# First mixture of experts: the up weights of a block in one 2 MB transfer

## The reference, cut to what matters

```
def expert_block(args):
    xb, ei = args
    hb = jax.nn.silu(xb @ w_gate[ei]) * (xb @ w_up[ei])      # 1024 -> 2 x 256
    return hb @ w_down[ei]                                   # 256 -> 1024
```

## Time and profile before

| | us |
|---|---|
| median of 3 runs | 2119.38 |
| lowest, highest | 2119.03, 2122.65 |
| span of the profiled execution | 2122.0 |
| PE busy in it | 1911.1 (90%) |
| DVE, ACT, POOL busy in it | 809.4, 501.7, 246.8 |

### The profile page before, as it was taken

The page is one execution under the profiler, slowest core; times in us unless marked ns, Lnnn a source line. Parts: engine busy times, 40 slices in busy tenths (PEclk is TensorE's granted clock), DMA queues, the critical chain, the costliest instruction groups (busy, mean ns, idle before and its releaser), DMA issues.

```text
span 2122.0 us, 26341 instructions
## 1 busy us (share of the span) xinstructions
PE 1911.1 (90%) x10372; PEld 1177.0 (55%) x10372; DVE 809.4 (38%) x1399; ACT 501.7 (24%) x868; POOL 246.8 (12%) x185
## 2 busy tenths in 40 slices
PE   9899999999989988999998998797978889797986
PEld 7777897785545567888987343332433333343433
DVE  5676454344634557558855110110201110120113
ACT  6656563331212145221224000000000000000002
POOL 4561520001111020003401000000000000000000
PEclk9999999989999999999999999999999999999999
DMA  7443441077999973312163999999999999999995
GB/s 292 159 157 138 184 157 60 1 289 303 421 423 422 417 299 127 129 57 100 60 258 138 418 417 421 413 422 412 422 416 419 419 415 422 412 421 413 421 416 198
DMA packets 123755, 630.67 MB, mean 297 GB/s; under 512 B 11708, under 2 KB 28476, under 8 KB 69021
## 3 DMA queue, kind: packets, MB, share of 16 engines
q1 hardware_dynamic: 109068, 598.65, 69.9%
q10 hardware_dynamic: 11216, 18.61, 2.3%
q0 software_dynamic: 3392, 12.32, 1.5%
HBM read 608.83 MB, written 20.71 MB: 297 GB/s over the span
## 4 chain that ended last, share of the span: by engine, by line
PE 53%; DMA 30%; DVE 6%; ACT 5%; POOL 2%; issue 2%; SPq 1%; POOLq 0%; ACTq 0%; DVEq 0%
PE psum L914 52%; DMA arena<-in_w 16%; DMA ring<-in_w 6%; DMA ring<-in_moe 4%; DMA in_spectra<-ring 2%; DVE arena L2216 2%; PE psum L912 1%; DVE weights_low L2208 1%; ACT weights_high L1754 1%; DVE arena L2208 1%; DMA arena<-in_stream 1%; ACT arena L1795 1%; SPq L614 1%; DMA arena<-x_rows,row_of 1%; ACT arena L1736 1%
## 5 line engine op out<-in xcount | busy, mean ns | idle before, releaser
L914 PE MATMUL psum<-ring,arena 128*64 128x512 f32 (+1 forms) x3064 | 688.3, 595 | 116.1 <-DMA ring<-in_w 87.3
L914 PEld LDWEIGHTS psum<-ring,arena 128*64 128x64 f32 x3064 | 227.9, 137 | 530.9 <-issue 522.0
L914 PE MATMUL psum<-arena 128*64 128x512 f32 (+5 forms) x1506 | 290.7, 457 | 28.5 <-DMA arena<-in_w 20.9
L1736 ACT ACTIVATE arena<-psum 128x512 f32<-128x512 f32 (+2 forms) x152 | 82.3, 550 | 722.6 <-PE psum L914 691.3
L914 PEld LDWEIGHTS psum<-arena 128*64 128x64 f32 (+2 forms) x1506 | 155.6, 166 | 171.6 <-issue 157.1
L914 PE MATMUL psum<-arena_low,weights_high 128*128 128x512 f32 (+1 forms) x704 | 249.3, 373 | 0.0
L914 PE MATMUL psum<-features_high_part,weights_high 128*128 128x512 f32 x576 | 228.3, 396 | 8.8 <-DVE weights_low L2208 3.0
L914 PE MATMUL psum<-features_high_part,weights_low 128*128 128x512 f32 x576 | 225.9, 392 | 0.0
L2216 DVE SCALAR_TENSOR_TENSOR arena<-psum,modp,arena 128x512 f32<-128x512 f32 x64 | 48.1, 751 | 319.2 <-PE psum L914 314.0
L2208 DVE TENSOR_TENSOR arena<-psum,arena 128x512 f32<-128x512 f32 (+2 forms) x48 | 28.9, 603 | 331.1 <-PE psum L914 255.5
L2208 DVE TENSOR_TENSOR weights_low<-ring,weights_high 128x2048 fp32r<-128x2048 f32 (+1 forms) x47 | 108.8, 2318 | 91.4 <-ACT weights_high L1754 87.8
(11 more groups left out here) (315 smaller groups left out, 1866.2 us busy)
## 6 DMA issues: line engine op xcount, KB each, us to landing
ring<-in_w SPq DMA_DIRECT2D x288, 1024.0 KB, 23.0
arena<-in_w SPq DMA_DIRECT2D x96, 1024.0 KB, 24.0
ring<-in_moe SPq DMA_DIRECT2D x93, 1024.0 KB, 20.3
ring<-in_stream SPq DMA_DIRECT2D x53, 1024.0 KB, 6.6
arena<-in_stream SPq DMA_DIRECT2D x16, 1024.0 KB, 4.9
in_spectra<-ring ACTq DMA_DIRECT2D x8, 1024.0 KB, 27.2
ring<-in_spectra SPq DMA_DIRECT2D x8, 1024.0 KB, 5.9
y_places<-arena ACTq DMA_DIRECT2D x15, 512.0 KB, 8.5
```

Source lines behind the costliest of these rows:

```text
L914: ins_ = pe.matmul(o, lhs, rhs, start=start, stop=stop)
L1736: bk.emptied.inc(act.activation(dst, o, func, **more))
```

## The change

The gate and up weights of a block come in one transfer of 2 MB instead of two of 1 MB. The array in HBM is the same. Seen as 256 rows of 8192 bytes (two halves of 128), partition q now takes rows 2q and 2q + 1, 16384 bytes in one run. Partition q < 64 so holds channels of the first four slices, and q >= 64 of the last four; which channel a partition holds is another one than before. To match it, `block_turned` picks every second channel of a slice (stride 2) and makes 16 products with the identity, 64 weight columns each, in place of eight transposes.

The nine slots become three of 2 MB for up weights and three of 1 MB for down weights, each with semaphores of its own (`s_upin`, `s_downin`). Block n waits for block n - 3 of its kind. SP's order in pair p is: the up weights of both blocks, then the down weights of the pair before. PE gives the slots of both blocks back when all of `up(p)` is done; `block_in(p + 2)` waits for that too. The filter tables are issued ahead of block 3's up weights. `moe1_uses` works out at which count of uses each block has been used. In pair 0 two small products follow `up`.

```
+    for e in range(experts_of(p)):
+        if 2 * p + e == UP_SLOTS:
+            filter_in()
+        up_in(2 * p + e)
     if p:
         for e in range(experts_of(p - 1)):
-            load(moe1_w[expert(p - 1, e), 2])
+            down_in(2 * p - 2 + e)
...
+def up_in(block):
+    if block >= UP_SLOTS:
+        sp.wait_ge(s_used, TURN["hyin"] + UP_USED[block - UP_SLOTS])
+    rows_ = moe1_w[expert(block), 0:2].rearrange("u p n -> (u p) n").rearrange("(q s) n -> q (s n)", s=2)
+    sp.dma_start(up_slot(block), rows_).then_inc(s_upin[block % UP_SLOTS], 16)
+    used.n += 1
+def down_in(block):
+    if block >= DOWN_SLOTS:
+        sp.wait_ge(s_used, TURN["hyin"] + DOWN_USED[block - DOWN_SLOTS])
+    sp.dma_start(down_slot(block), moe1_w[expert(block), 2]).then_inc(s_downin[block % DOWN_SLOTS], 16)
+    used.n += 1
...
 def block_turned(p):
-    k = 4 * half + j
-    mm(o[:, P * j:P * j + held], x_blk[p % 2][0:held, P * k:P * k + P], ident[0:held, 0:held],
-       True, True, bk_d if j == 3 else None, tr=True)
+    for h in range(2):
+        apart = x_blk[p % 2][0:held, 512 * h + P * j:512 * h + P * j + P].rearrange("t (q s) -> t s q", s=2)[:, half, :]
+        mm(o[64 * h:64 * h + 64, P * j:P * j + held], apart, ident[0:held, 0:held],
+           True, True, bk_d if j == 3 and h == 1 else None)
...
 def up(p):
+    for e in range(experts):
+        pe.wait_ge(s_upin[(2 * p + e) % UP_SLOTS], 16 * ((2 * p + e) // UP_SLOTS + 1))
     for k in range(KD):
-        if k % 4 == 0:
-            w = [unit() for _ in range(experts)]
...
-        if k % 4 == 3:
-            for _ in range(experts):
-                used()
+    for _ in range(experts):
+        used()
+    if p == 0:
+        keep_busy(begin(bk_d), 2)
...
 (POOL)
-    pool.wait_ge(s_used, TURN["hyin"] + first_up(p) + 1)
+    pool.wait_ge(s_used, TURN["hyin"] + UP_USED[2 * p])
     block_in(p + 2)
```

More of the change, by code:

```diff
@@ L61, with moe1_uses @@
 HIGH = 4
-MOE1_UNITS = 6 * PAIRS - 3
+BLOCKS = 2 * PAIRS - 1
+MOE1_UNITS = 2 * BLOCKS
+UP_SLOTS, DOWN_SLOTS = 3, 3
+def moe1_uses():
+    up_at, down_at, n = [], [], 0
+    for p in range(PAIRS + 1):
+        for at, q in ((up_at, p), (down_at, p - 1)):
+            for block in range(2 * q, min(2 * q + 2, BLOCKS)):
+                if block >= 0:
+                    n += 1
+                    at.append(n)
+    return up_at, down_at
+UP_USED, DOWN_USED = moe1_uses()
 HYOUT_SLOT = [5, 0, 1, 2]
@@ L110 @@
 ROOT_ROWS = ROWS_BACK + 2 * ST + 3 * KD + KD
-def first_up(p):
-    return 0 if p == 0 else 6 * p - 2
 VECS = [("conv", 32), ("head_g", 4), ("pool_scale", 4), ("ln_mix_g", 8), ("ln_mix_b", 8), ("ln_x_g", 8),
@@ L419, in build, with up_slot, down_slot @@
         y_blk = [arena[:, 5, 6 * FE + D * r:6 * FE + D * r + D] for r in range(2)]
+        def up_slot(block):
+            r = 2 * (block % UP_SLOTS)
+            return ring[:, r:r + 2, :].rearrange("p a n -> p (a n)")
+        def down_slot(block):
+            return ring[:, 2 * UP_SLOTS + block % DOWN_SLOTS, :]
         def row_stat(t, n, width=1):
@@ L563, in build @@
         s_xblk = [sem(f"block_in{r}") for r in range(2)]
-        s_arrived1 = [sem(f"moe1_arrived{r}") for r in range(RING1)]
+        s_upin = [sem(f"moe1_up_in{r}") for r in range(UP_SLOTS)]
+        s_downin = [sem(f"moe1_down_in{r}") for r in range(DOWN_SLOTS)]
         s_si1 = sem("silu1")
@@ L675, in _, with expert @@
             phase_a = turn[0]
[L676 to L682, removed]
+            def expert(block):
+                if block < NE:
+                    return block
+                return sp.value_load(spill_expert[0:1, block - NE:block - NE + 1], min_val=0, max_val=NE - 1)
+            def up_in(block):
[9 more added lines that the diff above has]
+                used.n += 1
             def window_in(q):
@@ L1313, in _ @@
             phase_a = turn[0]
-            arrived, turn[0] = s_arrived1, 0
             def block_turned(p):
@@ L1324, in block_turned @@
                     for j in range(4):
-                        k = 4 * half + j
-                        mm(o[:, P * j:P * j + held], x_blk[p % 2][0:held, P * k:P * k + P], ident[0:held, 0:held],
-                           True, True, bk_d if j == 3 else None, tr=True)
+                        for h in range(2):
+                            apart = x_blk[p % 2][0:held, 512 * h + P * j:512 * h + P * j + P]                                .rearrange("t (q s) -> t s q", s=2)[:, half, :]
+                            mm(o[64 * h:64 * h + 64, P * j:P * j + held], apart, ident[0:held, 0:held],
+                               True, True, bk_d if j == 3 and h == 1 else None)
                 note["x_blk", p] = bk_d.filled.n
@@ L1334, in up @@
                 experts = experts_of(p)
+                for e in range(experts):
+                    pe.wait_ge(s_upin[(2 * p + e) % UP_SLOTS], 16 * ((2 * p + e) // UP_SLOTS + 1))
+                w = [up_slot(2 * p + e) for e in range(experts)]
                 for k in range(KD):
-                    if k % 4 == 0:
-                        w = [unit() for _ in range(experts)]
                     for n in range(2):
-                        e, at = (n, 512 * (k % 4)) if experts == 2 else (0, 512 * (k % 4) + FE * n)
+                        e, at = (n, 512 * k) if experts == 2 else (0, 512 * k + FE * n)
                         mm(o[CAP * n:CAP * n + CAP, 0:256 * experts], x_blk_t[p % 2][:, k, CAP * e:CAP * e + CAP],
@@ L1361, in down @@
             def down(p):
-                w = [unit() for _ in range(experts_of(p))]
+                for e in range(experts_of(p)):
+                    pe.wait_ge(s_downin[(2 * p + e) % DOWN_SLOTS], 16 * ((2 * p + e) // DOWN_SLOTS + 1))
+                w = [down_slot(2 * p + e) for e in range(experts_of(p))]
                 pe.wait_ge(s_ea, note["hid_t", p])
```

## The result

| | us |
|---|---|
| median before, after (4 runs each) | 2121.02, 2152.59 |
| ratio, 95% interval | 1.013, 1.0108 to 1.0152 |
| the same kernel once more, beside the experiments | 1.0114, 1.0075 to 1.0152 |
| span before, after | 2122.0, 2151.7 |

One of the four runs of after was slow, 3246.92 us at a granted clock of 0.553; the median counts it (the other three are 2140.11, 2151.72 and 2153.46), the ratio does not. By the two ratios the change makes the kernel slower by 24 to 28 us. The forecast was 2137 with a range of 2122 to 2162; sign and range held, and the forecast difference, 17.6 us, was two thirds to three quarters of what came.

A forecast was written before the change was run, and what follows sets the result against it. The prediction took the first mixture to be bound by DMA bytes, 37.3 us a round, with PE 4.1 behind. Its terms -1.5 + 12.1 + 0 + 7 = +17.6 us onto the median 2119.38 gave 2137, range 2122 to 2162.

The forecast's parts named there:

- a start repaid at the end: Stage's end: with fewer loads queued the last two stores land sooner, the head start is made good: 2119, chance 0.09.
- PE's pace as a faster rival: Rounds of the first mixture: the queue could give more when asked, so PE paces the rounds: -18, 2102, chance 0.05.
- a rate above 430: DMA throughput in GB/s: named as a sign that the forecast is wrong; a rate above 424 was to decide for PE's pace.
- the cover holds: Rounds of the first mixture: only head start and rows count, +10.6 us, 2130, chance 0.22.
- the stores bind every round: Stores of spectra in the first mixture: each meets full turns, six rounds of 8.8 us and 10.6: +63, 2183, chance 0.08.
- Longer rows: Up weight loads: rows of 16384 bytes in place of 8192 make 62 MB about 1% cheaper, -1.5 us, bounds 0 and -4.6.
- Head start: Start of the first mixture: 3 MB less loaded ahead, +7.4 us, and SP resuming 4.7 us later: +12.1, bounds 7.4 and 15.
- `block_turned`, 2.2 us and hidden: PE's turning before up: 16 products take 2.2 us, +1.1 a pair, hidden by the loads, so 0.
- a turning without overlap: PE's block_turned: products do not run side by side, 4.4 us each, 39.9 a round: +29, 2148, chance 0.12.
- Less lookahead and stores, +7 in all: Rounds of the first mixture: less cover and late stores of spectra stall some rounds, 1.2 us each over six rounds.
- K settles at 3.0 us: Loop of landing, transfer and up: K, what was still queued, is 3.0 us, so the load queue stays filled in even runs.
- The turns of the stores: Stores of spectra alternating row by row with 16 KB load rows: land in 37.3 us, stalling PE at down by 8.6.

The follow-up runs named there:

- head_hold: Kernel before, but SP holds back after six 1 MB units, issues the filter tables and goes on only when up(0) has ended: ratio 1.0049, +10.4 us.
- eight_coarse: Kernel before with the held start, eight units of lookahead, and up waiting for all four units first and giving all back after its last product: ratio 1.0132, +28 us.
- halves: Changed kernel with each up load cut into two 1 MB transfers, second halves waited for only ahead of up's fifth slice, slots given back whole: ratio 1.0064, +13.6 us.
- two_transfers: Changed kernel with each up load cut into two 1 MB transfers of 8192-byte rows, its slots, waits and 16 products kept: ratio 1.0136, +28.8 us.
- transposes: Changed kernel with the eight transposes of before in block_turned in place of the 16 products: ratio 1.0134.
- numbers_ahead: Changed kernel, but SP reads a block's expert number, from block 16 on, before it waits for the slot: ratio 1.0102, +21.6 us.
- warm: Changed kernel with 12 small products on PE ahead of up's wait for weights in pairs 4, 6, 8, 10 and 12: ratio 1.0097, +20.6 us.
- downs_first: Changed kernel, but SP issues the first three down loads after the filter tables, ahead of block 3's up load: ratio 1.0142.
- combo: Changed kernel with downs_first, numbers_ahead and warm together, 2 MB loads kept: ratio 1.0121, +25.7 us.
- best: Changed kernel with halves, downs_first and numbers_ahead together, every load 1 MB in rows of 8192 bytes: ratio 1.0064, +13.6 us.

## Why the prediction was right or wrong

**What bounds it:** right for the kernel before. head_hold shows it: DMA time lost at the start is lost at the end. It also rules out the rival of a start repaid at the end, and PE's pace as a faster rival, since a queue that could give more when asked would have made the 10 us good. The sign I had named for that rival, a rate above 430, did appear: windows of 10 us with a PE wait in them reach 431 to 439 in after. They stay at 428 or below in before, head_hold, eight_coarse and halves, whose rows are all 8192 bytes, and of the six windows of 37 us of after from 520 us on none is above 423. So the sign was badly chosen. The rival that the cover holds (+10.6) falls by the time and by the waits over 4 us, the one that the stores bind every round (+63) by the time.

**Longer rows, -1.5 us:** not visible in the time; two_transfers costs no more than the changed kernel beyond the intervals. Fewer transfers, 0: right, by the same run. The fit of 2.0 us that the prediction takes from the Trainium skill (DMA: Bandwidth & Descriptors, section Anatomy of one DMA) is given there for transfers that POOL issues, and these loads are SP's; no such cost shows here.

**Head start, +12.1:** the mechanism was right, the size some 2 us too high. head_hold has +10.4. SP resumed at 495.90, not near 499.5 (to the earlier trace rows):

```profile
495.90 0.33 SPq L710 DMA_DIRECT2D ring<-in_moe  x1
```

That is 7.5 us after the start of `up(0)` in place of 4.5, so 2.9 us later and not 4.7: the longer turning ahead of `up(0)` did not push it back. With the 7.4 us of bytes this is 10.3, as in head_hold. The 13.0 us up to `up(3)` come near 12.1 by luck: in them are also an `up(1)` that took 2.2 us longer behind its wait of 8.3 us (I had said 7) and a wait of 1.7 us for DVE.

**`block_turned`, 2.2 us and hidden:** right, 1.92 us, and transposes brings nothing. The rival of a turning without overlap falls.

**Less lookahead and stores, +7 in all:** this term was mis-sized; it came out at 10.1 + 2.9 + 5.0 = 18.0 us in the profile, and at 14 to 17 by the ratios (24.2 and 27.6, less head_hold's 10.4). The step that failed is "K settles at 3.0 us: the queue doesn't run dry in an even run". I put the loop at 15.7 + K per pair against 18.7 us of bytes, and took the pairs as even. They aren't. In the round from 661.13 on, one pair is at PE's pace: from the end of `up` at 649.8 to the next end at 668.2, 18.4 us. The next is at the loop's: SP 1.2 us, landing 12.0, `up` 9.2 and 0.4 of sequencing, 22.8. Their sum, 41.2, is above the bytes' 37.3, and the queue idles in between. Three terms of the loop were wrong. SP's reading of the expert's number stands after the wait from block 16 on (1.2 us instead of none; numbers_ahead takes it out). `up` takes 9.2 us, not 7.1, because the clock has fallen during the wait (warm takes that out). And the landing was not 8.6 but 11 to 12 us. What of the 3 us more is the rest of the queue, the gather or the store of spectra I have not separated. Of the kernels that took single pieces numbers_ahead and warm gained 3 to 7 us, with intervals that overlap the changed kernel's, transposes and downs_first none; combo, with three of them, gained none either, but it pays for its small products, so whether the pieces add stays open. The cause that is shown is the demand for whole blocks beside a release of whole slots: eight_coarse has both and, apart from the held start and one slot less, nothing else that weighs; halves takes the demand alone away, and 15 us go with it.

**The turns of the stores:** the working fits, its place was wrong in all pairs but one. Turn by turn with 16 KB rows was worked out as 37.3 us, and the longest of combo has 37.1. In the changed kernel the median is 31.5 and the longest 33.8, short of the 37 I had named; its loads' queue is empty at times, which the text allowed for. And the wait that a late landing makes is in the rounds not at `down` but behind it, at `hidden_turned`: in combo `down` began on time, at 570.55, and the 5.2 us came after it. PE's four banks say the same, since the fill of four before a `down` is one of the pair before, and a down product or hidden values, no spectrum. So 3.65 us more of cover were there than I counted, and the 1.7 us in front of `down` in the earlier trace rows, which I read as the store's, have another cause; the profile names none, and the down weights, the other thing waited for there, are my guess. They come next in the queue behind the second halves: in before `down` starts at 670.67, 6.3 us after the second half of `up` could start, and 2 MB at 422 GB/s take 5.0. The exception is the end of the stage, where a whole spectrum is made in one pair and fills all four banks. There the longest store, 33.8 us, lies in the chain, and the `down` behind it waits 2.4 us for ACT's emptying, as forecast; this is part of the 5.0 us in the first table's last row.

```profile
775.40 5.05 PE L948 MATMUL psum<-ring,arena 128*64 128x512 f32 x16 [2.43 <-ACT ring L1774]
```

## What to carry over

A ring's depth in bytes did not tell the cost here: six units used by halves cost 14 us, eight used whole 28. Ask how much of the next step's data is asked for only when the current step ends, and whether the next step needs all of it before its first instruction. Here the same 9 MB cost 15 us more when a step waited for both halves at once, and a wait moved to the middle of the step gave them back without another slot. When such a loop is summed, sum each kind of step for itself: an average over unlike steps hides the one in which the queue runs dry. Merging transfers gained nothing that could be seen in this stage, which was already full of bytes, and it made the buffers coarser. And a remedy has its own price: products that keep the clock up cost their time when there is no wait to cover them.

## What the runs showed of the hardware

PE's granted clock was lower around the waits of 4 to 5 us for a load: part of the stretch is then at 1.2 instead of 2.4 GHz. In after, the windows around the waits for loads (the clock stands ahead of the DMA share) are

```profile
640.00:650.00 10.00, 9.56 (x39) 3.55 (x41) 0.00 (x0) 0.12 (x1) 0.00 (x0) 0.74 1.02 432
...
680.00:690.00 10.00, 8.21 (x30) 2.87 (x32) 0.00 (x0) 0.00 (x0) 0.00 (x0) 0.70 1.02 431
```

so that a wait of 4 us costs 2.1 us more in the `up` behind it (9.2 against 7.1). With small products under the wait the clock stayed at 1.00. A shorter wait had either outcome: after two waits of 2.4 us one `up` of after took 7.09 us and one 8.78, and in downs_first one took 7.09 after 3.7 us.

Two queues on the same DMA engines look as if they took turns by rows, not by bytes. The same store of 64 rows of 1 KB an engine took 27.3 us in the median beside 8 KB load rows in a full queue (before, halves, best), and 29.0 to 37.1 in combo, where half of the load rows have 16 KB. That is as far as these times can tell.
